# The prompt's attention in two halves of the PE array, query tiles from the longest to the shortest

## The reference, cut to what matters

```python
s_c = q @ k_cmp.T * scale + bias        # 63 compressed keys; valid if they end before the query
s_s = q @ k_slc.T * scale + bias        # all keys up to the query
s_w = q @ k_win.T * scale + bias        # keys of the last 512 positions
o_c = softmax(s_c) @ v_cmp;  o_s = softmax(s_s) @ v_slc;  o_w = softmax(s_w) @ v_win
return g[0] * o_c + g[1] * o_s + g[2] * o_w
```

## Time and profile before

| | |
|---|---|
| median of 3 runs | 4794.13 us (4792.4 to 4809.37) |
| profiled execution: its time, its span | 4797.22 us, 4795.4 us |
| stretch of `nsa_prompt` in the two layers | 335.1 and 317.8 us |
| PE, DVE, ACT, POOL busy, share of the span | 85%, 41%, 27%, 14% |

### The profile page before, as it was taken

The page is one execution under the profiler, slowest core; times in us unless marked ns, Lnnn a source line. Parts: engine busy times, 40 slices in busy tenths (PEclk is TensorE's granted clock), DMA queues, the critical chain, the costliest instruction groups (busy, mean ns, idle before and its releaser), DMA issues. The chain is left out here.

```text
span 4795.4 us, 58781 instructions
## 1 busy us (share of the span) xinstructions
PE 4076.8 (85%) x23204; PEld 3406.5 (71%) x23204; DVE 1961.7 (41%) x3875; ACT 1275.3 (27%) x2922; POOL 684.0 (14%) x495
## 2 busy tenths in 40 slices
PE   3899797787697799989969997967759789999897
PEld 2899676433465799987759996753336579999774
DVE  1333476523244433334442436763324353333354
ACT  0211255222222212113331114532212222121232
POOL 0035101233120000000000540013322010000000
PEclk9999899567798899999989998976879799999998
DMA  3334311300433222225532433121034222222554
GB/s 130 118 131 151 109 56 41 102 3 4 153 156 123 77 67 76 70 70 216 190 118 97 151 125 91 59 70 48 4 117 175 90 98 71 67 80 58 187 179 146
DMA packets 303623, 488.71 MB, mean 102 GB/s; under 512 B 64008, under 2 KB 234024, under 8 KB 298687
## 3 DMA queue, kind: packets, MB, share of 16 engines
q1 hardware_dynamic: 298730, 417.75, 26.9%
q0 software_dynamic: 4608, 67.11, 3.5%
HBM read 382.48 MB, written 117.95 MB: 104 GB/s over the span
## 5 line engine op out<-in xcount | busy, mean ns | idle before, releaser
L791 PE MATMUL ps<-h_hi,fu_hi 128*128 128x344 f32 x2112 | 680.5, 322 | 6.2 <-DVE fu_lo L831 6.2
L793 PE MATMUL ps<-h_hi,fu_lo 128*128 128x344 f32 x2112 | 676.6, 320 | 0.0
L792 PE MATMUL ps<-h_lo,fu_hi 128*128 128x344 f32 x2112 | 675.2, 320 | 0.0
L322 PE MATMUL ps<-zi_whi,h_hi 128*128 128x374 f32 x1440 | 487.0, 338 | 20.5 <-DVE h_lo L417 20.5
L323 PE MATMUL ps<-zi_wlo,h_hi 128*128 128x374 f32 x1440 | 482.6, 335 | 0.0
L324 PE MATMUL ps<-zi_whi,h_lo 128*128 128x374 f32 x1440 | 481.7, 335 | 0.0
L791 PEld LDWEIGHTS ps<-h_hi,fu_hi 128*128 128x128 f32 x2112 | 397.3, 188 | 9.4 <-DVE fu_lo L831 6.4
L793 PEld LDWEIGHTS ps<-h_hi,fu_lo 128*128 128x128 f32 x2112 | 398.6, 189 | 0.0
L792 PEld LDWEIGHTS ps<-h_lo,fu_hi 128*128 128x128 f32 x2112 | 397.3, 188 | 0.0
L946 PE MATMUL ps<-fd_whi,fd_fhi 128*128 128x512 f32 (+1 forms) x792 | 313.2, 395 | 41.7 <-DVE fd_flo L998 41.3
L947 PE MATMUL ps<-fd_wlo,fd_fhi 128*128 128x512 f32 (+1 forms) x792 | 311.6, 393 | 0.0
(11 more groups left out here) (589 smaller groups left out, 6945.4 us busy)
## 6 DMA issues: line engine op xcount, KB each, us to landing
fd_raw<-w_ffn_down SPq DMA_DIRECT2D x66, 1024.0 KB, 5.4
z<-zi_z SPq DMA_DIRECT2D x180, 187.0 KB, 1.9
zi_raw<-w_in SPq DMA_DIRECT2D x20, 1496.0 KB, 6.8
n_x<-z SPq DMA_DIRECT2D x64, 384.0 KB, 4.8
f_all<-fu_f SPq DMA_DIRECT2D x44, 516.0 KB, 3.4
fu_raw<-w_ffn_gate SPq DMA_DIRECT2D x44, 512.0 KB, 4.6
fu_raw<-w_ffn_up SPq DMA_DIRECT2D x44, 512.0 KB, 5.9
fd_f<-f_all SPq DMA_DIRECT2D x44, 384.0 KB, 3.3
```

Source lines behind the costliest of these rows:

```text
L322: nc.tensor.matmul(out, rows_hi, w_hi[:, i % 2, k], start=(k == 0), stop=False)
L791: nc.tensor.matmul(out, w_hi[f % 2][:, j, k, :], h_hi[:, k, seg], start=(k == 0), stop=False)
L792: nc.tensor.matmul(out, w_hi[f % 2][:, j, k, :], h_lo[:, k, seg], start=False, stop=False)
L793: m = nc.tensor.matmul(out, w_lo[f % 2][:, j, k, :], h_hi[:, k, seg], start=False, stop=(k == KD - 1))
```

## The change

It rewrites `nsa_prompt` and what feeds it:

- The window keys lie in partitions 0 to 63 and the selected keys in 64 to 127 of one tile `p_kT`; `p_qT` holds head h in the lower and head h+1 in the upper partitions (for the last slot the queries of head 0 are loaded a second time). Scores of the two branches use different row halves of the array and are written alternately.
- The values of a selected block go to partitions 0 to 63 of a bank and those of a window block to 64 to 127 of the same bank, so they use different column halves; the compressed branch has a bank of its own. Blocks are turned and multiplied in units of two.
- The exponentials are no longer scaled. POOL has no work in the stage; DVE multiplies the three outputs after they are transposed back (`outputs`), and adds them.
- The output of tile k is transposed and written during the first quarter of the next one.
- The tiles run from t = 7 down to t = 0 (`ORDER`).

```diff
-        self.kTs = sb("p_kTs", [HD, SEQ])
-        self.kTw = sb("p_kTw", [HD, SEQ])
-        self.qT = sb("p_qT", [HD, H, SEQ])
+        self.kT = sb("p_kT", [P, SEQ])
+        self.qT = sb("p_qT", [P, H, SEQ])
...
-    ldq(pd.zq[:], zr[:, NQ:NQ + 256].rearrange("(t p) n -> p t n", p=P))
+    ldq(pd.zq[:, :, 0:256], zr[:, NQ:NQ + 256].rearrange("(t p) n -> p t n", p=P))
+    ldq(pd.zq[:, :, 256:320], zr[:, NQ:NQ + HD].rearrange("(t p) n -> p t n", p=P))
...
-                        pe.wait_ge(S("q_ld"), 16)
+                        pe.wait_ge(S("q_ld"), 32)
...
+    ORDER = tuple(range(NT - 1, -1, -1))
...
+        for i in range(t + 1):
+            pairs.append((i * P, P, zk[:, i, 192:256], "s", i == 0, i == t))
+            if i < nw // P:
+                pairs.append((CW + i * P, P, zk[:, w0 // P + i, 320:384], "w", i == 0, i == nw // P - 1))
+        return [(CC, ncm, vc[0:ncm, :], "c", True, True)] + pairs
...
+    def unit(k, j):
+
+        return range(0, 1) if j == 0 else range(2 * j - 1, min(2 * j + 1, len(blocks(k))))
...
+                    qw = qT[0:HD, h, t * P:t * P + P]
+                    qs = qT[HD:P, (h - 1) % H, t * P:t * P + P]
+                    n = min(512, nk)
+                    nc.tensor.matmul(ps[:, 0, 0:n], qs, kT[HD:P, 0:n], start=True, stop=True)
                     n = min(512, nw)
-                    nc.tensor.matmul(ps[:, 2, 0:n], q, kTw[:, w0:w0 + n], start=True, stop=True)
+                    nc.tensor.matmul(ps[:, 2, 0:n], qw, kT[0:HD, w0:w0 + n], start=True, stop=True)
+                    if nk > 512:
+                        nc.tensor.matmul(ps[:, 1, 0:nk - 512], qs, kT[HD:P, 512:nk], start=True, stop=True)
...
+                        dst = ps[0:HD, 7, :] if kind == "c" else ps[0:HD, 6, :] if kind == "s" else ps[HD:P, 6, :]
+                        m = nc.tensor.matmul(dst, v, pT[0:n, g % 4, :], start=start, stop=stop)
...
+                for k in range(NT):
                     for h in range(H):
+                        if k + 1 < NT:
+                            scores(k + 1, h)
+                        if k and h == 0:
+                            outputs(k - 1)
+                        for j in quarter(k, h):
+                            if j < units(k):
+                                turns(k, j)
+                            if j:
+                                values(k, j - 1)
+                outputs(NT - 1)
...
-            @b.gpsimd
-            def _(pool):
-                for t in range(NT):
...
-                            m = nc.gpsimd.tensor_scalar(s[:, k, h, a:a + n], s[:, k, h, a:a + n], scl[:, k, h, br:br + 1], None, ALU.mult)
-                        m.then_inc(S("scaled"), 1)
```

More of the change, by code:

```diff
@@ L2226, in prompt_turns_act @@
             act.wait_ge(S("p_turned"), g + 1)
-            nc.scalar.activation(dst, ps[0:n, g % 3, :], ACT.Copy, scale=0.125 if kind >= 3 else 1.0).then_inc(S("p_read"), 1)
+            nc.scalar.activation(dst, ps[part, g % 3, :], ACT.Copy, scale=0.125 if kind >= 3 else 1.0).then_inc(S("p_read"), 1)
             g += 1
@@ L2316, in scores @@
[L2316 to L2335, removed]
-                        for h in range(H):
-                            m = nc.tensor.transpose(ps[:, 4 + g % 2, h * HD:h * HD + HD], yT[:, h * P:h * P + P], ident[0:HD, 0:HD])
-                    else:
-                        if i == 0:
[L2340 to L2343, removed]
+                        nc.tensor.matmul(ps[:, 3, 0:P], qw, kT[0:HD, w0 + 512:w0 + nw], start=True, stop=True)
@@ new lines, in scores, with turns @@
+                    nc.tensor.matmul(ps[:, 3, P:P + ncm], qw, kc[0:HD, 0:ncm], start=True, stop=True).then_inc(S("scored"), 1)
+                def turns(k, j):
+                    bl = blocks(k)
+                    for i in unit(k, j):
+                        g = first[k] + i
+                        if g >= 2:
+                            taken(pe, g - 2)
+                        if i == 0:
+                            pe.wait_ge(S("exped"), 4 * k + 4)
+                        col, n = bl[i][:2]
+                        for h in range(H):
+                            m = nc.tensor.transpose(ps[0:n, 4 + g % 2, h * P:h * P + P], s[:, k % 2, h, col:col + n], ident[:])
+                        m.then_inc(S("turned"), 1)
@@ new lines, in values @@
+                def values(k, j):
+                    bl = blocks(k)
+                    for i in unit(k, j):
+                        g = first[k] + i
+                        col, n, v, kind, start, stop = bl[i]
+                        taken(pe, g)
+                        dst = ps[0:HD, 7, :] if kind == "c" else ps[0:HD, 6, :] if kind == "s" else ps[HD:P, 6, :]
+                        m = nc.tensor.matmul(dst, v, pT[0:n, g % 4, :], start=start, stop=stop)
+                        if i == 0:
+                            m.then_inc(S("c_summed"), 1)
+                        if i == len(bl) - 1:
+                            m.then_inc(S("y_summed"), 1)
@@ new lines, in take, with copies @@
+                    link(V.tensor_scalar(neg[:, k % 2, h, :], mx[:, k % 2, h, :], -1.0, None, ALU.mult), S("maxed"))
+                def copies(k, h):
+                    bl = blocks(k)
+                    for j in quarter(k, h):
+                        for i in (unit(k, j) if j < units(k) else ()):
+                            g = first[k] + i
+                            if g % 2 == 1:
+                                dve.wait_ge(S("turned"), g + 1)
+                                n = bl[i][1]
+                                V.tensor_copy(pT[0:n, g % 4, :], ps[0:n, 4 + g % 2, :]).then_inc(S("odd"), 1)
```

211 lines of the change are left out of this document (104 added, 107 removed).

## The result

The changed kernel takes 4604.07 us (median of 4 runs, 4592.99 to 4604.74), the one before 4796.01 in the same rounds (4792.4 to 4809.37): **a ratio of 0.9589, 95% interval 0.9566 to 0.9613**. The profiled execution took 4603.99 us; its span is 4602.2, 193.2 less than before.

The account below looks back on a forecast made before the run. Bound: a chain per quarter (scores, take, exponentials, copy, turn, values). 28 + 147.8 + 58 + 4 = 238 us, 245 with a slower clock, saves 81.4 a layer; less 1.7 each for queries, forecast 4635 us, range 4600 to 4715.

Parts of the forecast that it names:

- the sum: Predicted steps of the stage added up, 245 us a layer with the clock allowance, giving 4637.8 us for the profiled execution.
- start: Stage start, longest tile uncovered: four heads' scores and take, then the last exponentials, 28 us.
- tiles 7 to 4, with four tile ends: Four quarters each of scores, take, exponentials, copy, turn, values: 147.8 us; each tile end 0.6 for outputs.
- tiles 3 to 0, with three: Short tiles, some quarters only PE's work: 22, 16, 12 and 8, together 58 us; each tile end 0.6.
- clock at 0.68: PE idles more, so its granted clock falls from 0.725 to 0.68 and its 105 us a layer grow by 7.
- second query load: The duplicated queries' load lies on the path: bounds 0.9 and 2.55 us, taken as 1.7 in each layer.
- B: Rival: PE passes keep strict order, three for a pair instead of two; 4690 us, chance 0.13.
- C: Rival: nothing overlaps in the array halves, 4755 us, chance 0.06; only the column halves fail, 4697, 0.08.
- E: Rival: changes between whole array, row halves and column halves empty the array; slower, 4820 us or above, chance 0.03.
- D: Rival on PE's clock: 1.2 GHz throughout gives 4715 us, chance 0.08; 2.4 GHz throughout gives 4570, 0.04.
- POOL's wait: At the tile's end, the first turn's 6.36 us wait for POOL's scaling of the last head goes.
- The values' pairs: Selected and window value products in column halves: 30 pairs a layer, each 1.18 us instead of 2.36.

Follow-up runs that it names:

- e9: The e2 kernel plus unused products of 64 rows by 64 columns on the upper row half ahead of selected and window score products: 4932.84 us, ratio 1.03.
- e13: The e2 kernel plus unused products shaped like the real ones (64 by 128) on the upper row half, in the start and tiles 7 to 5: 4705.49 us.
- e4: The changed kernel plus five unused 512-column products behind the scores of the first tile, in the stage's start: 4598.5 us, ratio 0.9589.
- e2: The changed kernel without row halves, both key sets and the queries in partitions 0 to 63: 4725.09 us, ratio 0.9864.
- e15: The fastest follow-up kernel (4474.51 us; copies moved earlier, filled start) with DVE's output instructions ahead of the next tile's first take: 4499.61 us.
- e5: The kernel before, with POOL multiplying one column instead of the whole row, outputs not the reference's: 4793.56 us, ratio 1.0001.

## Why the prediction was right in kind and 31 to 38 us too high

The profiled execution is 33.8 us below the sum's 4637.8, 17 a layer. By its steps, in the mean of the two layers:

| step | predicted | measured |
|---|---|---|
| start | 28 | 28.5 |
| tiles 7 to 4, with four tile ends | 147.8 + 2 | 148.6 |
| tiles 3 to 0, with three | 58 + 2 | 53.0 |
| clock at 0.68 | +7 | none: 0.84 and 0.79 |
| second query load | 1.7 | 0.1 |

- **Right**: pairs run side by side in both kinds of halves (the first pass of each starts within 10 ns; four passes of values, two pairs of them, take 1.08 us at the higher level, at 3175.65 of the quarter above), and a quarter of tile 7 takes 9.2 to 10.5 us where the sum had 10.08. Rivals B, C and E are out. Of D, the clock, the unlikely side had the direction: 2.4 GHz throughout, 4570, 0.04. Of a change of mode the runs show about 0.2 us at 1.2 GHz: in e9 two passes and a change take 1.90 us (922.30 to 924.20), where two passes of like products take 1.71 in e13 (890.40 to 892.11). That is the size from which the prediction excluded rival E. The Trainium skill, "TensorEngine Tiling (Array Packing)", Key Properties, says that a change of tiling mode drains the array; the 64*64 and 64*128 products that run in turn agree with it. The Trainium skill, "TensorE: Matmul & The Clock Gate", Part 3, has matmuls start in program order; in the changed kernel's timeline the second product's first pass starts with the first product's first, 0.53 us ahead of the first one's second, so for products of two passes the measurement decides against the strict reading.
- **The step that failed: "I do not trust the clock of before to hold: at 0.68 ... the 105 us of it that are PE's grow by 7".** The direction was wrong. It rested on idling lowering the clock. PE does idle for more of the stage (28 and 26% of it, 19 and 22% before), and the clock rose all the same, to 0.84 and 0.79. Pauses do hold the clock down, as the starts of e4 and of the changed kernel show (0.89 against 0.56). What the prediction left out is the other influence: e13 shows that the second half of the array at work raises it, and e2, without row halves, ran at 0.67, close to the 0.68 that was allowed for the pairs. Undoing the allowance is 7 a layer. The sum's own 0.725 was too low by the same mistake: the short tiles, most of them PE's work, took 51.1 us at 0.96 and 54.9 at 0.90 where the sum had 60 at 0.725. As an estimate from e13's slope (7.5 us for 0.1 of clock in a piece of 108 us), 0.2 of clock over half as long a piece is 7 us. That makes about 14 of the 17 us a layer, half of it by this estimate.
- **The second query load**, "I take 1.7, in each layer", cost 0.1 us: below the lower bound of 0.9. That is 1.6 of the 17 us. Both bounds counted the load as if the present one ended on the path with nothing to spare.
- **Tiles 7 to 4 came out within 2 us, but this is in part luck, errors that offset each other**: the clock there was 0.85 and 0.81, and e13 says that in such tiles a higher clock mostly lengthens PE's waits. The tile ends were 9.0 us of waiting, not 4, and in e15 the edit that takes this wait away makes the kernel slower.
- **POOL's wait**, whose end the prediction counted on, was worth nothing by itself in the kernel before (e5). The sum for the new quarters never used the 6.36 us, so the number wasn't hurt.
- **The halves' shares were off both ways.** The values' pairs entered as 1.0 us of each quarter, 16 a layer in tiles 7 to 4 alone, and were worth 4.3 a layer: most of their time was not on the path. The row halves were worth more than their passes: with the clock that rises with them, 58 a layer.

Open: how much of the 58 us is the clock's and how much the passes'. By the tiles 4 to 0 of e13, 0.1 of clock is worth 7.5 us of 108; no run here holds the clock while the passes change. Open too: of the 192 us, the row halves account for 121 and the column pairs for 8, and the order of the tiles and POOL's work had no effect that the runs show. Some 60 us are left for what no run took away by itself: the units of two blocks, the factors computed once a tile, and the output moved into the next quarter.

## What to carry to other kernels

Write down the chain of one period through all engines, and look first at what stands in each queue between two of its links: swapping two calls in one engine's list (89 us) was worth nearly half of the rewrite (192), and together with one more swap on DVE it decided whether the column pairs were worth 8 us or 38. A long wait for one engine is no limit until it is shown that the other inputs of the waiting instruction are ready earlier: most of POOL's 19 us moved to ACT and DVE. When two products move into two halves of the array, reckon with a changed granted clock, and don't carry the old one over.

## What the hardware did that wasn't expected

- The granted clock rose when unused products kept the second half of the array at work beside the same real products, with PE busy for less time: 0.72 to 0.82 over 139 us, 0.50 to 0.70 in the start. In the changed kernel's own start, with both halves at work and longer pauses, it stayed at 0.56 and 0.50.
- Products of 64*64 and 64*128 in different row halves don't overlap, those of one shape do: 3.90 against 1.71 us from pair to pair.
- Five unused products in a start of waits raised the clock there from 0.56 to 0.89 in layer 1 (0.50 to 0.82 in layer 2), and in the dense order the whole stage ran at 0.95 and 0.94 instead of 0.87.
